# A hybrid DeltaNet and window-attention layer on one core: x transposed before its norm, the first two tiles together, split decays, and the last rows stored one by one

## The chip, the cores and the metric

One core of one Trainium2 chip. The metric is the device time of one execution in microseconds (us); the numbers given for a kernel are medians over several executions. TensorE is the matrix engine (PE in the profile; its weight loads are PEld), VectorE is DVE, ScalarE is ACT, GpSimd is POOL, SyncE is SP. SP issues the weight transfers; ScalarE issues the transfers of x, the constants and the output.

## The reference: what is computed

```python
h = rms_norm(x, norm_w)                       # x: 2048 x 1024, fp32
z = h @ w_in                                  # all branches' inputs
# branch A: gated DeltaNet, 8 heads of 128, chunks of 64
q, k, v = silu(causal_conv(z_qkv)); q, k = l2_normalize(q), l2_normalize(k)
g = -exp(a_log) * softplus(a + dt_bias)
gc = cumsum(g) within a chunk
decay = exp(gc[i] - gc[j]) for i >= j         # per head and chunk
o = chunked delta rule(q, k, v, decay, beta)
ya = (rms_norm(o) * silu(z_a)) @ w_o_a
# branch B: window attention, 16 heads of 64, sinks, relative bias
yb = (attention(q, k, v) * silu(z_b)) @ w_o_b
y = x + (sigmoid(gate_a) * ya + sigmoid(gate_b) * yb) @ w_out
out = rms_norm(y, final_norm_w)
```

## The kernel before, in words

The sequence is done in 4 blocks of 512 tokens (`TB`), each as 4 rows of 128 (`NT`); the model width of 1024 is 8 slices of 128 (`KT`). Every fp32 operand of a large product is held as a high part in fp32r and a low part that is the rest, and a product is three fp32r matmuls (`split_mm`, L1118 to L1122). The weights are 91 tiles of 128 x 1024. In block 0 each tile is read raw by SP (`load_raw`, L344), its high part made by ScalarE (`high_part`, L447), its low part by POOL (`low_part`, L376), and both parts saved to memory; blocks 1 to 3 read the saved parts back. There are three weight slots (`SLOTS`). A 128x512 tile product (`gemm_steps`, L1131) is 8 slices of three matmuls, 24 in all, and takes 24 x 0.227 = 5.45 us; it fills one of two PSUM banks, which must have been read (`z_read`) before it is filled again.

The order of the work is written out by hand, engine by engine; engines meet at semaphores, and an engine that waits holds up all that stands behind it in its own program.

**Front (block 0).** ScalarE issues the load of x (L437) and the constants (L440 to L445), makes the high parts of tiles 0 to 2 (L453), squares x (`square_x`, L475) and makes `nea` (L487). VectorE takes the mean (L776), POOL the power -0.5 (L393), and VectorE scales the four rows of x in place (L779). TensorE then transposes x in 8 slices of four (`transpose_x`, L1158), VectorE evicts each with the norm weight into `h32` (L789), ScalarE makes its high part (`h_high`, L482) and VectorE its low part (`h_low`, L796). TensorE runs the three tiles "pro" one after the other: the first waits slice by slice for h. Between the second and the third it transposes the first one's result for beta and the decays (`beta_decay`).

**Heads.** In `head` (L1196) TensorE's own work for a head is mixed with steps of the next head's six tile products (`fill`). It starts with the sums of the decays: POOL makes `g_up`, the mask UPTO times the head's g (`decays`, L395 to L398), and one fp32 matmul of the mask AFTER by `g_up` gives the exponents (L1207). Its result is waited for by ScalarE (exp, L625) and, as leave to overwrite `g_up`, by POOL. Then come transposes of k and q (L1203), the products k k and k q (L1214), the transposes of v, 8 fill steps, the doubling levels (`square`, `apply`), the logits (L1267) of the attention, whose block-diagonal q (`qbd`) ScalarE wrote in the head before (L566, L567) into one of two buffers, and the four chained steps of the state. The head's output is transposed in L1348, just ahead of the next head's L1207.

**Block ends.** After the heads come 16 gate tiles (6 inside the last head), 8 "ya", 8 "yb", 3 "pro" and 8 "out" tiles. ScalarE issues the load of the next block's x after the last head and squares it after gate tile 8; VectorE scales it; TensorE transposes 6 slices after gate tile 14 and 2 within "ya" (L1380 to L1388).

**Tail.** The last 8 tiles give 4 rows x 2 halves. VectorE adds each half to x (L1101) when the half's last tile is done, ScalarE squares the 4 rows (L754), VectorE takes the mean (L1107), POOL the power, VectorE scales the rows (L1110), and one 2 MB transfer stores them (L760).

## Time and profile before

| | us |
|---|---|
| median of 3 runs | 2855.15 (2854.82 to 2855.34) |
| the profiled execution | 2855.39 |
| its span, first to last instruction | 2853.6 |
| TensorE busy | 2779.8 (97%) |
| VectorE busy | 1408.7 (49%) |
| ScalarE busy | 956.1 (34%) |
| POOL busy | 410.5 (14%) |
| TensorE's mean granted clock | 0.997 |
| transfers | 463.12 MB, 162 GB/s |

The span leaves out 1.8 us of the execution around it. Times in the trace count from the span's start. "Busy" is the union of the recorded instructions; matmuls overlap each other, so their pace is read from the distance of their starts, not from their durations. In a row of the timeline the bracket at the end says how long the engine had sat idle before it and which instruction ended that.

### The profile page before, as it was taken

How to read it: one execution, taken by the hardware profiler on the slowest of the kernel's cores; microseconds unless marked ns; L12 is line 12 of the kernel's file. 1: busy time of each engine (PE TensorE's matmuls, PEld its weight loads, DVE VectorE, ACT ScalarE, POOL GpSimd, SP SyncE). 2: the span in 40 equal slices, each digit the busy share in tenths (PEclk: the TensorE clock that was granted, in tenths of full speed). 3: DMA queues.
4: the chain of work that ended last, by engine and by line, in shares of the span. 5: the costliest groups of instructions: out<-in, count | busy, mean ns of one | idle time of the engine just before them, and what ended most of it. 6: DMA issues, size and time to landing. Idle time of an engine off the chain costs nothing.

```text
span 2853.6 us, 48812 instructions
## 1 busy us (share of the span) xinstructions
PE 2779.8 (97%) x19624; PEld 2279.9 (80%) x19624; DVE 1408.7 (49%) x3173; ACT 956.1 (34%) x2961; POOL 410.5 (14%) x237
## 2 busy tenths in 40 slices
PE   5999999999999999999999999999999999999997
PEld 4877777788888888888888888888888888888885
DVE  4577667523166666622226666652224666664022
ACT  3444444432233434331113434432112344333100
POOL 3333233343201000100001000100000001100000
PEclk9999999999999999999999999999999999999998
DMA  6545444488643333345553323325555233323553
GB/s 218 186 162 185 140 158 159 171 306 317 237 166 123 106 116 113 119 164 216 195 215 122 116 106 121 123 105 192 209 189 210 106 121 121 108 107 118 202 207 137
DMA packets 77552, 463.12 MB, mean 162 GB/s; under 512 B 13072, under 2 KB 17296, under 8 KB 29200
## 3 DMA queue, kind: packets, MB, share of 16 engines
q1 hardware_dynamic: 65520, 429.42, 42.1%
q10 hardware_dynamic: 11808, 30.57, 2.9%
q8 instruction: 157, 2.57, 0.4%
q14 instruction: 67, 0.55, 0.1%
HBM read 356.15 MB, written 103.81 MB: 161 GB/s over the span
## 4 chain that ended last, share of the span: by engine, by line
PE 84%; issue 8%; DVE 5%; POOL 1%; ACT 1%; DMA 1%; DVEq 0%; POOLq 0%; SPq 0%; ACTq 0%
PE bank L1120 21%; PE bank L1122 20%; PE bank L1121 20%; PE bank L1240 5%; PE bank L1229 3%; PE bank L1267 2%; PE bank L1214 2%; PE bank L1282 1%; PE bank L1203 1%; PE bank L1274 1%; PE bank L1330 1%; PE bank L1335 1%; PE bank L1325 1%; PE bank L1320 1%; PE bank L1338 1%
## 5 line engine op out<-in xcount | busy, mean ns | idle before, releaser
L1120 PE MATMUL bank<-hT_hi,w_sl 128*128 128x512 f32 x2144 | 904.7, 422 | 12.2 <-DVE za L854 10.7
L1122 PE MATMUL bank<-hT_hi,w_sl 128*128 128x512 f32 x2144 | 840.3, 392 | 0.0
L1121 PE MATMUL bank<-hT_lo,w_sl 128*128 128x512 f32 x2144 | 837.7, 391 | 0.0
L1120 PEld LDWEIGHTS bank<-hT_hi,w_sl 128*128 128x128 f32 x2144 | 404.0, 188 | 92.0 <-issue 23.2
L1122 PEld LDWEIGHTS bank<-hT_hi,w_sl 128*128 128x128 f32 x2144 | 402.3, 188 | 89.8
L1121 PEld LDWEIGHTS bank<-hT_lo,w_sl 128*128 128x128 f32 x2144 | 405.1, 189 | 58.4
L380 POOL TENSOR_TENSOR w_sl<-w_raw,w_sl 128x1024 fp32r<-128x1024 f32 x91 | 229.0, 2519 | 455.1 <-ACT w_sl L453 455.0
L872 DVE SCALAR_TENSOR_TENSOR area<-zraw,stc,area 128x512 f32<-128x512 f32 x288 | 234.5, 814 | 3.3
L393 POOL TENSOR_TENSOR rqo<-qo,half 128x8 f32<-128x8 f32 x32 | 52.4, 1638 | 1017.0 <-DVE qo L1023 1017.0
L771 DVE TENSOR_SCALAR area<-bank 128x256 f32<-128x256 f32 (+1 forms) x192 | 81.0, 422 | 237.9 <-PE bank L1240 196.8
L1240 PE MATMUL bank<-area 64*64 64x128 f32 (+1 forms) x3072 | 162.4, 245 | 0.0
L1006 DVE SCALAR_TENSOR_TENSOR s_cur<-s_cur,scs,bank 128x128 f32<-128x128 f32 x128 | 44.4, 347 | 230.7 <-PE bank L1335 230.7
L617 ACT ACTIVATE area<-bank 128x256 f32<-128x256 f32 x160 | 61.5, 384 | 253.2 <-PE bank L1229 253.0
L1240 PEld LDWEIGHTS bank<-area 64*64 64x64 f32 x3072 | 134.7, 134 | 11.7 <-issue 11.7
L1229 PEld LDWEIGHTS bank<-area 64*64 64x64 f32 x2560 | 87.1, 134 | 58.0 <-issue 54.8
L453 ACT ACTIVATE w_sl<-w_raw 128x1024 fp32r<-128x1024 f32 x91 | 96.1, 1056 | 77.6 <-PE bank L1122 47.7
L541 ACT ACTIVATE zraw<-bank 128x512 f32<-128x512 f32 x96 | 56.8, 591 | 170.6 <-PE bank L1122 167.7
L1070 DVE SCALAR_TENSOR_TENSOR area<-area,bank 128x512 f32<-128x512 f32 x28 | 19.3, 688 | 185.9 <-PE bank L1122 185.9
L536 ACT ACTIVATE area<-area 128x512 f32<-128x512 f32 x96 | 60.0, 625 | 149.7 <-DVE area L872 149.7
L1229 PE MATMUL bank<-area 64*64 64x64 f32 x2560 | 109.0, 224 | 0.3 <-ACT area L621 0.3
L667 ACT ACTIVATE o_sb<-bank,scs 128x128 f32<-128x128 f32 x128 | 46.7, 365 | 170.1 <-PE bank L1325 170.0
L1120 PE MATMUL bank<-w_sl,oa_hi 128*128 128x512 f32 x256 | 100.6, 393 | 0.0
(192 smaller groups left out, 4565.0 us busy)
## 6 DMA issues: line engine op xcount, KB each, us to landing
w_sl<-saved_w SPq DMA_DIRECT2D x273, 1024.0 KB, 4.8
saved_w<-w_sl SPq DMA_DIRECT2D x91, 1024.0 KB, 4.8
w_raw<-in_w_tiles SPq DMA_DIRECT2D x91, 512.0 KB, 5.9
area<-in_x ACTq DMA_DIRECT2D x8, 2048.0 KB, 10.0
out_y<-area ACTq DMA_DIRECT2D x4, 2048.0 KB, 7.2
bias_sb<-in_bias ACTq DMA_DIRECT2D x33, 128.0 KB, 3.1
fw<-in_final_w ACTq DMA_DIRECT2D x1, 512.0 KB, 10.5
stc<-in_step_const ACTq DMA_DIRECT2D x32, 6.5 KB, 2.4
```

Source lines behind the costliest of these rows:

```text
L380: pool.tensor_tensor(w_sl[:, s, 1, :], w_raw[:, f % 2, :], w_sl[:, s, 0, :].bitcast(F32), ALU.subtract).then_inc(lo_ready, 1)
L453: act.activation(w_sl[:, s, 0, :], w_raw[:, f % 2, :], ACT.Copy).then_inc(hi_ready, 1)
L536: act.activation(ez[i % 2], qkv[:, par, i, :], ACT.Tanh, scale=0.5).then_inc(tanh_z[i], 1)
L617: act.activation(p_sb[l % 2], pv(bank[5]), ACT.Copy).then_inc(p_ready, 1)
L771: return dve.tensor_scalar(dst, src, 1.0, None, ALU.mult)
L872: ins = dve.scalar_tensor_tensor(acc, zraw[:, i, k:k + TB], stc[:, par, CONV * i + k:CONV * i + k + 1], acc, ALU.mult, ALU.add)
L1120: pe.matmul(dst, a_hi, b_hi, start=first, stop=False)
L1121: pe.matmul(dst, a_hi, b_lo, start=False, stop=False)
L1122: return pe.matmul(dst, a_lo, b_hi, start=False, stop=last)
L1214: ins = pe.matmul(dst[:, t, :], k[:, c], src[:, c], start=True, stop=True)
L1229: ins = pe.matmul(pv(bank[5])[lo:hi, t, :], ptt[lo:hi, t, 0:CH], p_sb[(l - 1) % 2][lo:hi, t, :], start=True, stop=True)
L1240: ins = pe.matmul(bch(6)[lo:hi, t, c0:c1], p_sb[(l - 1) % 2][lo:hi, t, :], ptt[lo:hi, t, c0:c1], start=True, stop=True)
```

## The change

x comes in four loads of one row each, for block 0 two from SP (ahead of the weights) and two from ScalarE. TensorE transposes the raw x. The reciprocal root is put on a diagonal (`diag_x`, VectorE), multiplied by the mask of ones (`rstd_broadcast`, one fp32 128x512 matmul into bank 7), copied to SBUF by ScalarE (`rstd_rows`) and multiplied in when `h32` is evicted. The transposes use five banks instead of six. In the front the squares come first, the first two tiles are computed together, slice by slice, and the constants' loads shrink to four. g is split into `g_hi` and `g_lo`; POOL makes two masked products, and two fp32r matmuls take the place of the fp32 one. `qbd` has one buffer instead of two. In the last block, rows are added, squared, scaled and stored one by one.

```diff
-        qbd = sb("qbd", [P, 2, NC, P])
+        qbd = sb("qbd", [P, NC, P])
+        after_r = sb("after_r", [P, P], F32R)
+        g_hi = sb("g_hi", [P, NT, H], F32R)
+        g_lo = sb("g_lo", [P, NT, H])
+        gu = sb("gu", [P, 2, NT, P], F32R)
...
-        g_up = chunks(scratch(0))
+        g_up = [gu[:, 0, :, :], gu[:, 1, :, :]]
-        junk_q, junk_k = chunks(scratch(7)), chunks(scratch(9))
+        junk_q, junk_k = chunks(scratch(4)), chunks(scratch(9))
+        zflat = zraw[:, :, :].rearrange("p i t -> p (i t)")
+        diag_x = chunks(zflat[:, 0:TB])
+        rstd_x = zflat[:, D:D + TB]
...
SP:
+            for t in (2, 3):
+                sp.dma_start(x_sb[:, t, :], x[0][:, t, :]).then_inc(x_landed[t], 16)
             load_raw(0)
             load_raw(1)
POOL:
-            def decays(par, n1):
+            def decays(h, n1):
                 pool.wait_ge(sc_ready, n1)
-                pool.tensor_tensor(g_up, mk[:, UPTO:UPTO + 1, :].to_broadcast([P, NT, P]),
-                                   scs[:, par, G, :, None].to_broadcast([P, NT, P]), ALU.mult).then_inc(gup_ready, 1)
+                pool.wait_ge(g_split, (n1 - 1) // H + 1)
+                for up, g in zip(g_up, (g_hi[:, :, :].bitcast(F32), g_lo[:, :, :])):
+                    ins = pool.tensor_tensor(up, mk[:, UPTO:UPTO + 1, :].to_broadcast([P, NT, P]),
+                                             g[:, :, h, None].to_broadcast([P, NT, P]), ALU.mult)
+                ins.then_inc(gup_ready, 1)
...
+            power(st4[:, 4:8], st4[:, 8:12], NT, x_mean, 1, x_rstd)
             low(SLOTS)
-            power(st4[:, 4:8], st4[:, 8:12], NT, x_mean, 1, x_rstd)
...
+                    for t in range(NT):
+                        power(sty[:, 4 + t:5 + t], sty[:, 8 + t:9 + t], 1, row_mean, t + 1, row_rstd)
ScalarE:
+            def load_x(j, ts=range(NT)):
+                for t in ts:
+                    act.dma_start(x_sb[:, t, :], x[j][:, t, :]).then_inc(x_landed[t], 16)
+            load_x(0, (0, 1))
             act.dma_start(mk[:, :, :], masks).then_inc(const_in, 16)
...
-            act.dma_start(bias_sb[:, 0, :, :], bias[0]).then_inc(const_in, 16)
-            act.dma_start(fw[:, :], final_w).then_inc(const_in, 16)
-            for n in range(SLOTS):
-                high_part(n)
...
+            def rstd_rows(j):
+                act.wait_ge(bc_done, j + 1)
+                act.activation(rstd_x, bank[7][:, :], ACT.Copy).then_inc(bc_ready, 1)
             square_x(0)
+            high_part(0)
+            high_part(1)
+            rstd_rows(0)
+            for k in range(KT):
+                h_high(0, k)
+            high_part(2)
...
             act.activation(nea[:, :], db[:, 0, :], ACT.Exp).then_inc(const_ready, 1)
+            act.dma_start(fw[:, :], final_w).then_inc(fw_in, 16)
...
+                after(act, lg_done[1], n1 - 1)
+                act.activation(qbd[0:DH, :, 0:CH], zq[0:DH], ACT.Copy, scale=DH ** -0.5)
+                act.activation(qbd[DH:P, :, CH:P], zq[DH:P], ACT.Copy, scale=DH ** -0.5).then_inc(z_read[bk], 1)
...
+                act.wait_ge(ssq_ready[0], n1)
                 p_copy(0)
                 act.wait_ge(ksc_ready, n1)
                 scaled(kd, bch(3), ksc, kd_ready)
-                act.wait_ge(ssq_ready[0], n1)
...
                     if more and j == FILL_GATES + 2:
                         square_x(b1)
+                if more:
+                    rstd_rows(b1)
...
+                if not more:
+                    for t in range(NT):
+                        act.wait_ge(half_added, t + 1)
+                        act.activation(junk_y[:, 0:TB], y_out[:, t, 0:TB], ACT.Square, accum_out=sty[:, 12 + t:13 + t]).then_inc(row_ssq, 1)
+                        act.wait_ge(row_ssq, t + 1)
+                    for t in range(NT):
+                        act.wait_ge(row_added, t + 1)
+                        act.activation(junk_y[:, TB:D], y_out[:, t, TB:D], ACT.Square, accum_out=sty[:, t:t + 1]).then_inc(row_ssq, 1)
+                        act.wait_ge(row_ssq, NT + t + 1)
+                    for t in range(NT):
+                        act.wait_ge(row_final, t + 1)
+                        act.dma_start(out[b][:, t, :], y_out[:, t, :]).then_inc(y_stored, 16)
+                    break
VectorE:
                 dve.wait_ge(x_rstd, j + 1)
-                for t in range(NT):
-                    ins = dve.tensor_scalar(x_sb[:, t, :], x_sb[:, t, :], st4[:, 4 + t:5 + t], None, ALU.mult)
-                ins.then_inc(x_normed, 1)
+                dve.tensor_tensor(diag_x, mk[:, IDENT:IDENT + 1, :].to_broadcast([P, NT, P]),
+                                  st4[:, 4:8, None].to_broadcast([P, NT, P]), ALU.mult).then_inc(x_diag, 1)
...
+                dve.wait_ge(bc_ready, j + 1)
-                dve.tensor_scalar(h32[k % 2], bank[2 + k % 6][:, :], nw[:, k:k + 1], None, ALU.mult).then_inc(h32_ready, 1)
+                dve.scalar_tensor_tensor(h32[k % 2], bank[2 + k % 5][:, :], nw[:, k:k + 1], rstd_x, ALU.mult, ALU.mult).then_inc(h32_ready, 1)
...
+            dve.tensor_scalar(after_r[:, :], mk[:, AFTER, :], 1.0, None, ALU.mult).then_inc(dve_init, 1)
...
+                ch.link(dve.tensor_scalar(g_hi[:, :, :], sc_all[:, G, :, :], 1.0, None, ALU.mult))
+                dve.tensor_tensor(g_lo[:, :, :], sc_all[:, G, :, :], g_hi[:, :, :].bitcast(F32), ALU.subtract).then_inc(g_split, 1)
...
+                    for t in range(NT):
+                        add(t, 0, half_added)
+                        if t == 1:
+                            dve.wait_ge(half_added, 2)
+                    for t in range(NT):
+                        if t < NT - 1:
+                            dve.wait_ge(out_part, t + 1)
+                        else:
+                            dve.wait_ge(tile_done, USE["out", b, 2 * NT - 1] + 1)
+                        add(t, 1, row_added)
+                        if t:
+                            mean(t - 1)
+                        if t > 1:
+                            final(t - 2)
+                    mean(NT - 1)
+                    final(NT - 2)
+                    final(NT - 1)
+                    break
TensorE:
+            def rstd_broadcast(j):
+                pe.wait_ge(x_diag, j + 1)
+                pe.matmul(bank[7][:, :], mk[:, ONES, :], diag_x.rearrange("p t c -> p (t c)"), start=True, stop=True
+                          ).then_inc(bc_done, 1)
...
-                pe.matmul(bank[5][:, :], mk[:, AFTER, :], g_up.rearrange("p t c -> p (t c)"), start=True, stop=True
+                pe.matmul(bank[5][:, :], after_r[:, :], g_up[0].rearrange("p t c -> p (t c)"), start=True, stop=False)
+                pe.matmul(bank[5][:, :], after_r[:, :], g_up[1].rearrange("p t c -> p (t c)"), start=False, stop=True
                           ).then_inc(dec_done, 1)
...
-            pe.wait_ge(x_normed, 1)
+            for k in range(5):
+                transpose_x(0, k)
+            rstd_broadcast(0)
+            n = USE["pro", 0, 0]
+            pair = (gemm_steps(n, hT_hi, hT_lo), gemm_steps(n + 1, hT_hi, hT_lo))
             for k in range(KT):
-                transpose_x(0, k)
-            n = USE["pro", 0, 0]
-            gemm(n, hT_hi, hT_lo, True)
-            gemm(n + 1, hT_hi, hT_lo)
+                if k < KT - 5:
+                    transpose_x(0, k + 5)
+                pe.wait_ge(h_hi, k + 1)
+                pe.wait_ge(h_lo, k + 1)
+                for steps in pair:
+                    next(steps)
+            for steps in pair:
+                next(steps, None)
...
                     if more and j == GATE_TILES - 2:
-                        pe.wait_ge(x_normed, b + 2)
-                        for k in range(6):
+                        pe.wait_ge(ot_read, (b + 1) * H)
+                        for k in range(5):
                             transpose_x(b + 1, k)
+                        rstd_broadcast(b + 1)
...
-                    if more and c in (1, 2):
+                    if more and c < KT - 5:
                         transpose_x(b + 1, c + 5)
```

## Rows read from the trace of the kernel before

**Rows 1.** Page, part 4: the chain that ended last, by engine.

```profile
PE 84%; issue 8%; DVE 5%; POOL 1%; ACT 1%; DMA 1%; DVEq 0%; POOLq 0%; SPq 0%; ACTq 0%
```

**Rows 2.** Windows: heads of block 0 and of block 1 (stretch: length, busy of each).

```profile
88.00:565.00 477.00, 456.40 (x3818) 369.18 (x3817) 322.95 (x689) 223.00 (x700) 164.37 (x79) 1.00 0.47 161
807.00:1260.00 453.00, 452.52 (x3821) 370.19 (x3820) 272.40 (x690) 179.69 (x652) 41.18 (x31) 1.00 0.32 115
```

**Rows 3.** Waits of PE: two of block 0's heads, the only one of block 1's.

```profile
PE bank L1120 <- DVE za L854: 10.7, 7, 1.5
PE bank L1330 <- DVE r_sb L1000: 5.1, 8, 1.7
...
PE bank L1335 <- ACT y_sb L670: 0.5, 1, 0.5
```

**Rows 4.** Timeline of the front (start us, us, what, idle before).

```profile
19.38 1.06 ACT L453 ACTIVATE w_sl<-w_raw 128x1024 fp32r<-128x1024 f32 x1 [6.21 <-DMA w_raw<-in_w_tiles]
20.34 1.04 ACT L475 ACTIVATE zraw<-area 128x1024 f32<-128x1024 f32 x1
20.51 2.35 POOL L380 TENSOR_TENSOR w_sl<-w_raw,w_sl 128x1024 fp32r<-128x1024 f32 x1 [4.93 <-ACT w_sl L453]
25.12 0.17 DVE L776 TENSOR_SCALAR st<-st 128x4 f32<-128x4 f32 x1 [25.12 <-ACT zraw L475]
29.31 5.89 PE L1158 MATMUL bank<-mk,area 128*128 128x128 f32 x32 [29.31 <-DVE area L779]
30.51 0.75 DVE L789 TENSOR_SCALAR za<-bank,nw 128x512 f32<-128x512 f32 x1 [1.27 <-PE bank L1158]
...
40.20 0.63 ACT L482 ACTIVATE hT_hi<-zb 128x512 fp32r<-128x512 f32 x1
40.87 0.69 DVE L796 TENSOR_TENSOR hT_lo<-zb,hT_hi 128x512 fp32r<-128x512 f32 x1
...
48.33 0.48 PE L1120 MATMUL bank<-hT_hi,w_sl 128*128 128x512 f32 x1
```

**Rows 5.** DMA view of the first 60 us: rate in 40 slices, issues to landing.

```profile
GB/s 0 248 377 385 404 395 406 240 295 360 279 254 429 426 355 93 437 188 336 0 0 0 0 0 0 0 0 0 0 0 11 126 399 197 328 262 339 205 334 1
...
w_raw<-in_w_tiles SPq DMA_DIRECT2D x7, 512.0 KB, 6.0
area<-in_x ACTq DMA_DIRECT2D x1, 2048.0 KB, 9.5
```

**Rows 6.** Timelines of DVE and ScalarE's queue in the tail.

```profile
2833.31 2.48 DVE L1101 TENSOR_TENSOR area<-bank,area 128x512 f32<-128x512 f32 x4 [19.42 <-PE bank L1122]
...
2841.84 4.87 DVE L1110 SCALAR_TENSOR_TENSOR area<-area,sty,fw 128x1024 f32<-128x1024 f32 x4 [1.12 <-POOL sty L393]
...
2846.80 0.35 ACTq L760 DMA_DIRECT2D out_y<-area  x1
```

**Rows 7.** Timeline of PE at the start of a head of block 1.

```profile
1146.46 0.60 PE L1348 MATMUL bank<-mk,area 128*128 128x128 f32 x4
1146.90 1.02 PE L1207 MATMUL bank<-area,mk 128*128 128x512 f32 x2
1147.76 1.04 PE L1203 MATMUL bank<-mk,area 128*128 128x128 f32 x8
...
1153.16 0.39 PE L1121 MATMUL bank<-hT_lo,w_sl 128*128 128x512 f32 x1
1153.39 0.39 PE L1122 MATMUL bank<-hT_hi,w_sl 128*128 128x512 f32 x1
```

**Rows 8.** Timeline of POOL and DVE in the same head.

```profile
1157.37 1.04 POOL L397 TENSOR_TENSOR area<-mk,scs 128x512 f32<-128x512 f32 x1 [4.13 <-DVE scs L771]
1157.44 1.26 DVE L868 TENSOR_SCALAR area<-zraw,stc 128x512 f32<-128x512 f32 x1
...
1160.81 0.42 DVE L771 TENSOR_SCALAR area<-bank 128x256 f32<-128x256 f32 x1 [2.12 <-PE bank L1240]
```

**Rows 9.** Timeline of DVE at the start of a head of block 0.

```profile
147.98 2.73 DVE L1042 TENSOR_TENSOR oa_lo<-za,oa_hi 128x512 fp32r<-128x512 f32 x1
```

107 lines of the change are left out of this document (68 added, 39 removed).

## The prediction, made blind

> **What bounds the kernel now.** I read the page first: in the chain that ended last TensorE holds 84% [rows 1]. A share like that hides which stages have slack, so next comes the table by stage [rows 2]. In block 1's heads (807 to 1260 us) TensorE works 452.52 of 453 us; in block 0's heads (88 to 565) only 456.40 of 477. So there are three kinds of time: the front before the first product and the tail after the last, where TensorE idles; block 0, where it waits for others; and the rest, where only TensorE's own work counts. The waits say for whom block 0 waits: VectorE's SiLU of za 10.7 us in 7 waits, r_sb 5.1 us in 8; block 1 has 0.5 us in all [rows 3].
>
> A change of less than 0.2% (5.7 us) is no change for a measurement of this kernel.
>
> **Front.** Today ScalarE converts weight tile 2 (19.38) before it squares x, because its program has the conversions first; x has long landed: its load takes 9.5 us from its issue at 0.74 [rows 4, 5]. Then four squares from 20.34, the mean at 25.12, power, the four scalings of x, transposes from 29.31, the first h32 at 30.51, the last low part of h ends at 41.56, both first tiles are done at about 48, and tile 2 starts at 48.33 [rows 4].
>
> After the change the step is built up as follows.
> - x: the same 2 MB, now ahead of the weights on both queues. The DMA slices run at some 380 to 400 GB/s [rows 5], so 2 MB take about 5.3 us of transfer. I estimate the first quarter at 6.8 and the last at 9.3 us; the bounds are 5 and 10.3 (today's landing of the whole).
> - Four squares take 25.12-20.34 = 4.8: from 6.8 to 11.6; I take 12.
> - Mean 0.2, power 1.0, one 128x512 product on VectorE 0.7, one fp32 128x512 matmul 0.9 (priced below), one ScalarE copy 0.6, and 0.1 for each of five hand-overs: 3.9, so the first h32 comes at 16. ScalarE's two weight conversions (2 x 1.06) fit into the time in which it waits for that matmul. The raw transposes of slices 0 to 4 are done by then. POOL now does the power ahead of all low parts, so low part 1 ends near 18.2.
> - Eight slices take 41.56-30.51 = 11.05 us [rows 4]: VectorE sets the pace at 1.38 us a slice. The eviction becomes a scalar_tensor_tensor with one PSUM and one SBUF input; its nearest row is 0.69 against 0.75 now (the residual add, 2.48 for four, a pitch of 0.6 [rows 6]), so I count no change. I add 1 us, since low part 1 on POOL now overlaps the chain and VectorE can be stretched by POOL (below). End: 28.
> - The pair of tiles eats six matmuls a slice, 6 x 0.227 = 1.36 us, just VectorE's pace, so both tiles end 1.4 us later, 29.5. Today the second tile needs 5.45 us more, after the first.
> - What is late next: tile 2's weights. Its conversion stands behind the last h_high on ScalarE, so 27.3+1.06 = 28.4, and its low part takes 2.4 (L380) after a short hand-over: 30.9. Tile 2 starts at 31.0, and I allow 0.5 us for TensorE's start: **31.5 instead of 48.33, a gain of 16.8 us.**
>
> That allowance is the soft spot. TensorE's granted clock is 1.00 throughout the front, yet its 32 first transposes take 5.9 us, 0.18 us each, where four later ones take 0.44, 0.11 each [rows 4, 7]: 2 us are lost after the idle 29 us. If it starts at half pace once more between the transposes and the gemm, the pair lags up to 2.5 us, since six matmuls a slice at half pace cost 2.7 us against VectorE's 1.38; the lower bound takes that in. The Trainium skill ("TensorE: Matmul & The Clock Gate", What's actually happening) says that an idle array falls back to 1.2 GHz and needs sustained work to rise again. By that rule the pair would start at 1.2 GHz and tile 2 at about 33. The first transposes agree with it; no row shows a short gap.
>
> The front's gain holds only if the following weights keep up: raw tile 4 is issued after low part 2 (31.3), lands 6.0 later [rows 5], is converted and split by 40.8, and is wanted at 31.5+2 x 5.45 = 42.4. It fits by 1.6 us. After that TensorE is bound as before to its 88.15. Bounds of the whole: 13 and 20 us.
>
> **Decays.** One fp32 matmul 128x512 (two records) holds TensorE from L1207 at 1146.90 to L1203 at 1147.76: 0.86 us. An fp32r matmul of the same shape starts every 0.227 us (1153.16, 1153.39) [rows 7]. Two of those are 0.455, saving **0.40 us a head.** I cost the change of type before and after at nothing, since the gemm's matmuls stand between fp32 ones at every turn already. In blocks 1 to 3 TensorE has no slack, so 24 heads give 9.7.
>
> POOL pays: two 1.04 products a head instead of one. VectorE feels it: an L868 that begins beside POOL's L397 takes 1.26 us and ends 0.3 us after it; a second product holds it 1.04 us longer. But VectorE then sits idle for 2.12 us before its next step [rows 8], which covers it. At a block's start nobody waits for the product today: block 1's list has no such wait [rows 3]. The Trainium skill ("GPSIMD Engine Reference", Specifications) has the two engines share their SBUF interfaces, in contention when VectorE's instruction has two SBUF inputs or a 2-port mode. By that rule L868 loses 1.04 us in all 24 heads; the sum stays the same while the idle 2.12 us cover it.
>
> In block 0 seven heads wait at the first fill matmul for VectorE (1.5 us each) [rows 3]. VectorE's delay starts at the output transposes, ahead of the decay matmul, so those heads gain nothing; head 0 gains 0.4. There the second product falls where VectorE reads PSUM, so I cost it at zero. Sum for decays: **10.0 us**, bounds 6 (each block 0 head loses half of a product) and 13 (all 32 gain).
>
> **Block boundaries.** VectorE's four scalings go, one product, one ScalarE copy, three more DMA issues come; all hidden, since TensorE does nine gate tiles of 5.45 us between the load's issue and its first transposes and never waits there. The new wait for the broadcast row stands ahead of h32, which is wanted only by the next "pro" tiles, dozens of microseconds later. TensorE has one more fp32 128x512 matmul: 3 x 0.86 = **2.6 us lost.** Transposes stay 32, five slices ahead and three later. The single qbd buffer adds a wait on ScalarE for the second logits of the head before; in its program order it already waited for later work (probs of the second half), so zero. The ssq_ready wait ahead of p_copy is for ScalarE's own older work: zero.
>
> **Tail.** TensorE ends at T = 2833.3, where VectorE's wait ends; today four adds (2.48), four squares, mean and power (to 2841.84), four finals (4.87), then a 2 MB store issued at 2846.80 and ended with the span at 2853.6: 20.3 us [rows 6]. Afterwards only row 3 is left at T: add 0.7, then VectorE's mean of row 2 and final of row 1 to T+2.3, mean of row 3 to 2.75, final of row 2 to 3.95 (its power is ready at 2.4), final of row 3 (power ready at 3.9) to 5.2. The 512 KB store: 2 MB take 6.8 us, less 1.5 MB at 400 GB/s that is 2.9; a raw tile of 512 KB behind another transfer takes 6.0 [rows 5]. I take 3.7, nearer the first, since only row 2 is ahead of it. Started at 5.3 it lands at T+9.0. **Gain 11.3 us**, bounds 9 and 12.1. TensorE's own halt for the first half's adds shrinks by 0.1.
>
> **Sum.** 16.8 + 10.0 - 2.6 + 11.3 = 35.5 us off the profiled execution's 2855.39, which stands 0.24 over the median of the runs: 2819.9, so **2820 us**.
>
> **Rivals.**
> - The front is held by DMA and a slow TensorE: x lands late, weights arrive late, gain 10 instead of 16.8: 2827. For it: the landing is 9.5 us at nearly full DMA shares. 15%.
> - Block 0 gains too: less waiting on VectorE's chain because everything there shifts; 7 x 0.4 more, and the front at 18: 2816. 12%.
> - fp32r is no cheaper here (0.43 each, as the fp32 records): the change doesn't do what it says, and 10 us are missing: 2830. Against it the 0.227 of all other fp32r matmuls. 2%.
> - POOL's second product is not covered: each head loses a full 1.04 us, 32 x 1.04 = 33: 2853, no change. Against it the 2.12 us. 4%.
> - Slower: the same place, but POOL and VectorE stretch each other. It decides at a delay of 2.12+35.5/32 = 3.2 us a head; at 3.7 a head loses 1.6, 51 us in all: 2871. For it: in block 0 a VectorE subtraction takes 2.73 instead of 0.69 (the front's h low part has it) while POOL's low parts run [rows 9]. Against it: L397 is a third as long as two low parts. 2%.
>
> My forecast has the remaining 65%. The range holds it and the first three rivals, as well as the bounds summed, 13+6-2.6+9 = 25.4 to 20+13-2.6+12.1 = 42.5 us of gain: 2812 to 2830. Faster: 65+15+12+2 = 94%; within 0.2%: 4%; slower: 2%.
>
> **What would show it.** Tile 2's start near 31.5; L1207's records half as wide, the next transposes 0.46 us after them, and a head's period in blocks 1 to 3 shorter by 0.4; block 0's wait for za longer by 0.4; L868 at 2.3 us without a new wait of TensorE; store of row 3 at T+5.3. I am wrong if TensorE shows new waits in blocks 1 to 3, or if weights stop it between 31 and 88 us.

## The result: 2833.5 us instead of 2855.2, and where the forecast's other 13.5 us went

| | before | after |
|---|---|---|
| median | 2855.24 (2854.82 to 2855.52, 4 runs) | 2833.51 (2827.68 to 2836.23, 4 runs) |
| ratio | | 0.9921, 95% interval 0.9909 to 0.9933 |
| the profiled execution, its span | 2855.39, 2853.6 | 2835.45, 2833.6 |

The change makes the kernel faster by 21.7 us. The forecast was 2820 with a range of 2812 to 2830: the sign was right, the size was not. The four runs of the changed kernel also lie 8.5 us apart, those of the kernel before 0.7. That spread is the first clue: something in the new kernel comes out now one way and now the other. TensorE's mean granted clock goes with it: 0.998 in the run of 2827.68, 0.997 in that of 2831.58, 0.996 in the other two, 2835.45 and 2836.23. The profiled execution is thus one of the slower ones.

The page of the changed kernel, parts 1 and 4:

```profile
PE 2783.0 (98%) x19632; PEld 2288.2 (81%) x19632; DVE 1406.3 (50%) x3177; ACT 958.6 (34%) x2973; POOL 450.7 (16%) x272
...
PE 92%; DVE 4%; ACT 1%; issue 1%; DMA 1%; POOL 1%; ACTq 0%; DVEq 0%; SPq 0%
```

TensorE holds 92% of the chain instead of 84% [rows 1], as it should where front and tail shrink. But its busy time rose from 2779.8 to 2783.0, although the decay matmuls became cheaper. Busy time of an engine that does less can only rise if some of its work ran slower.

**Where the 20.0 us of the span came from.** I compared the start of the decay matmul of each head (L1207 before, L1303 after). It is earlier by 10.9 us in head 0, 11.35 in head 1 and 11.37 in head 2, and then the lead melts: 9.98, 8.60, 8.65, 7.27 and 5.61 in heads 3 to 7 of block 0, and 2.81 at the first head of block 1 (804.39 against 807.20). From there it grows by 0.38 in most heads, loses 0.6 at each of the two block boundaries, and is 8.9 at TensorE's last matmul; the tail adds 11.1.

| | forecast | measured in the profiled executions |
|---|---|---|
| front, to the third tile | 16.8 | 10.9 |
| block 0, from its first decay matmul to block 1's (with the first boundary) | 0.4 - 0.9 | -8.1 |
| blocks 1 to 3, with two boundaries | 9.7 - 1.7 | 6.1 |
| tail | 11.3 | 11.1 |
| sum | 35.5 | 20.0 |

**Block 0.** The view of PE's waits between 77 and 555 us of the changed kernel:

```profile
PE bank L1211 <- DVE za L908: 13.8, 7, 2.2
PE bank L1427 <- DVE r_sb L1054: 5.0, 8, 1.7
```

The wait for za is 13.8 us in 7 instead of 10.7 [rows 3], 0.44 a head longer. That is the forecast's own term: the cheaper decay matmul of these heads is waited away. But 7 x 0.4 only explains that nothing is gained. The rest is in the windows by stage (length, busy of PE, PEld, DVE, ACT, POOL, granted clock, DMA share, GB/s):

```profile
77.20:550.00 472.80, 451.48 (x3757) 367.49 (x3756) 315.17 (x677) 219.03 (x690) 168.27 (x84) 0.98 0.46 159
...
198.00:200.50 2.50, 0.64 (x3) 0.58 (x4) 2.50 (x4) 1.84 (x12) 2.50 (x2) 1.00 0.50 206
200.70:203.00 2.30, 2.30 (x8) 1.79 (x7) 1.48 (x4) 0.00 (x0) 1.99 (x2) 0.56 1.08 235
```

Block 0's mean granted clock (the number ahead of the DMA share, which stands second from the end) is 0.98, where it was 1.00 [rows 2]; in block 1 it is 1.00. In the head that starts at 194 us it reads 1.00 while TensorE idles, then 0.56. In matmuls, from PE's timeline of the same head:

```profile
199.86 0.47 PE L1211 MATMUL bank<-hT_hi,w_sl 128*128 128x512 f32 x1 [1.94 <-DVE za L908]
...
202.05 0.63 PE L1212 MATMUL bank<-hT_lo,w_sl 128*128 128x512 f32 x1
202.48 0.63 PE L1213 MATMUL bank<-hT_hi,w_sl 128*128 128x512 f32 x1
```

From 201.2 to 204.2 the matmuls start 0.43 us apart, and from 204.5 on 0.23 again: TensorE runs at 1.2 GHz for 3 us, 1.3 us after an idle of 1.94 us has ended. The head is then 61.08 us long instead of 59.66; three others are as long (61.06 to 61.35), and the last one loses as much. The kernel before idled 1.53 us at the same place and its clock read 1.00 there. So the saving of 0.4 us did not merely come to nothing; it made the idle longer (1.91 to 2.21 us), and in five of seven heads the longer idle was followed by some 3 us at half pace; in the two others, after idles of 1.92 and 1.91, it was not. At this point that is a reading of one trace, and it is what the first experiment tests.

The idle itself is VectorE's and POOL's. Their timelines in that head:

```profile
195.94 5.42 POOL L401 TENSOR_TENSOR w_sl<-w_raw,w_sl 128x1024 fp32r<-128x1024 f32 x2 [3.82 <-ACT w_sl L480]
201.67 1.38 POOL L414 TENSOR_TENSOR rk<-ssk,half 128x4 f32<-128x4 f32 x1 [0.31 <-DVE ssk L955]
```

```profile
196.38 2.73 DVE L1096 TENSOR_TENSOR oa_lo<-za,oa_hi 128x512 fp32r<-128x512 f32 x1
199.04 0.68 DVE L908 SCALAR_TENSOR_TENSOR za<-area,bank 128x512 f32<-128x512 f32 x1
```

VectorE's oa_lo is 2.73 as before [rows 9], and za, for which TensorE waits, stands right behind it. The arithmetic is telling: the first of POOL's two low parts ends near 195.94 + 2.4 = 198.3, and oa_lo, which takes 0.69 undisturbed, ends 0.7 after that. It did not run slower, it stood until POOL's instruction was over. The SiLU of za, which has one input in PSUM, takes 0.68 beside the second low part. The Trainium skill ("SBUF — State Buffer", SBUF: two separate sides) says just that: whichever of the two engines starts first holds the shared ports for its whole instruction, and the other blocks. The trace agrees, 2.73 against 0.69.

**Front.** The timelines of ScalarE, POOL, VectorE and PE, in order of time:

```profile
10.21 1.06 ACT L499 ACTIVATE zraw<-area 128x1024 f32<-128x1024 f32 x1 [2.17 <-DMA area<-in_x]
13.97 4.53 PE L1254 MATMUL bank<-mk,area 128*128 128x128 f32 x20 [13.97 <-DMA db<-in_decay_bias]
14.48 1.02 POOL L414 TENSOR_TENSOR st<-st,half 128x4 f32<-128x4 f32 x1 [10.75 <-DVE st L826]
15.47 5.10 POOL L401 TENSOR_TENSOR w_sl<-w_raw,w_sl 128x1024 fp32r<-128x1024 f32 x2
15.54 2.83 DVE L828 TENSOR_TENSOR zraw<-mk,st 128x512 f32<-128x512 f32 x1 [1.21 <-POOL st L414]
18.43 1.92 PE L1243 MATMUL bank<-zraw,mk 128*128 128x512 f32 x2
21.08 0.75 DVE L839 SCALAR_TENSOR_TENSOR za<-bank,nw,zraw 128x512 f32<-128x512 f32 x1 [2.71 <-ACT zraw L505]
...
31.32 0.69 DVE L846 TENSOR_TENSOR hT_lo<-zb,hT_hi 128x512 fp32r<-128x512 f32 x1
...
37.43 0.48 PE L1211 MATMUL bank<-hT_hi,w_sl 128*128 128x512 f32 x1
```

The first h32 comes at 21.08, forecast 16. Row 1 of x landed only at 10.2, so the squares end 2 us late; the diagonal is 2.83 instead of 0.7, since POOL's low part began 0.07 us ahead of it; the broadcast is 1.92 instead of 0.9, at half pace. From the first h32 to the last low part it takes 10.9, as forecast (11.05, and 1 allowed). But then the pair of tiles is not done: it began at 23.3, ran at half pace to about 26.4 and ended at 36.9, so the third tile starts at 37.43, forecast 31.5.

**Blocks 1 to 3** behave mostly as forecast (6.1 instead of 8.0). PE at the start of the head at 1141 us:

```profile
1141.42 0.60 PE L1445 MATMUL bank<-mk,area 128*128 128x128 f32 x4
1141.78 0.48 PE L1303 MATMUL bank<-gu,after_r 128*128 128x512 f32 x1
1142.10 0.39 PE L1304 MATMUL bank<-gu,after_r 128*128 128x512 f32 x1
1142.33 1.04 PE L1299 MATMUL bank<-mk,area 128*128 128x128 f32 x8
```

From L1303 to the next transposes it is 0.55, where it was 0.86 [rows 7], and 0.36 instead of 0.44 from L1445 to L1303: 0.39 a head together. POOL's second product and VectorE beside it:

```profile
1152.33 1.05 POOL L420 TENSOR_TENSOR gu<-mk,g_hi 128x512 fp32r<-128x512 f32 x1 [4.12 <-issue]
1153.34 1.23 POOL L420 TENSOR_TENSOR gu<-mk,g_lo 128x512 fp32r<-128x512 f32 x1
```

```profile
1152.40 1.25 DVE L922 TENSOR_SCALAR area<-zraw,stc 128x512 f32<-128x512 f32 x1
1155.40 0.42 DVE L821 TENSOR_SCALAR area<-bank 128x256 f32<-128x256 f32 x1 [1.74 <-PE bank L1337]
```

VectorE's product is stretched by the first of POOL's two and by no more than before [rows 8]: 1.25, not the 2.3 that were forecast, and 1.26 at most in all heads of blocks 1 to 3. It idles 1.74 us afterwards, and TensorE has no new wait. What is missing there is the seventh head of each of these blocks, 0.35 us longer in its state steps for a reason that I did not find, and 0.34 us of a late weight load in block 3.

**Tail.** The timelines of VectorE and of ScalarE's queue around TensorE's last matmul, which ends at 2824.4:

```profile
2823.94 1.28 DVE L1164 SCALAR_TENSOR_TENSOR area<-area,sty,fw 128x1024 f32<-128x1024 f32 x1
2825.13 0.69 DVE L1154 TENSOR_TENSOR area<-bank,area 128x512 f32<-128x512 f32 x1
```

```profile
2826.66 3.89 ACTq L800 DMA_DIRECT2D out_y<-area  x4
```

The final of row 0 begins just before TensorE ends and holds the last add back by 0.7 us; still the span ends 9.2 us after TensorE, instead of 20.3 [rows 6].

### The profile page after: what moved, and what is told of

Same layout as the page of the kernel before. It is cut to its first block, busy times and chain, and to the rows that moved or that the text cites. A ratio compares the mean times of both kernels' runs of the same rounds, so it can differ in the third digit from the quotient of the medians.

```text
span 2833.6 us, 48983 instructions
## 1 busy us (share of the span) xinstructions
PE 2783.0 (98%) x19632; PEld 2288.2 (81%) x19632; DVE 1406.3 (50%) x3177; ACT 958.6 (34%) x2973; POOL 450.7 (16%) x272
## 4 chain that ended last, share of the span: by engine, by line
PE 92%; DVE 4%; ACT 1%; issue 1%; DMA 1%; POOL 1%; ACTq 0%; DVEq 0%; SPq 0%
PE bank L1211 24%; PE bank L1213 22%; PE bank L1212 22%; PE bank L1337 5%; PE bank L1326 3%; PE bank L1364 2%; PE bank L1311 2%; PE bank L1379 1%; PE bank L1371 1%; PE bank L1299 1%; PE bank L1427 1%; PE bank L1432 1%; PE bank L1417 1%; PE bank L1422 1%; PE bank L1435 1%
## 5 line engine op out<-in xcount | busy, mean ns | idle before, releaser
L1211 PE MATMUL bank<-hT_hi,w_sl 128*128 128x512 f32 x2144 | 909.2, 424 | 14.7 <-DVE za L908 13.8
L414 POOL TENSOR_TENSOR sty<-sty,half 128x1 f32<-128x1 f32 (+1 forms) x7 | 7.1, 1020 | 612.9 <-DVE sty L1198 424.8
L1211 PE MATMUL bank<-oa_hi,w_sl 128*128 128x512 f32 x256 | 100.6, 393 | 0.0
```

The lines of the kernel that those rows point to most:

```text
L414: pool.tensor_tensor(dst, src, half[:, 0:n], ALU.pow).then_inc(ready, 1)
L1211: pe.matmul(dst, a_hi, b_hi, start=first, stop=False)
```

## The experiments

The question was what holds block 0 and the front back. Theory C: the longer idle of TensorE lets the granted clock fall. Its rivals: the cost of the decays' own parts, POOL's queue, or VectorE's order of work. All ran beside the kernel before, whose median was 2855.5 to 2855.7 each time; ratios are to it, of four executions unless it is said otherwise. A median alone says little here where the clock varies: the changed kernel's own runs reach from 2827.7 to 2836.2. So the traces decide.

### 1. Two spare matmuls in block 0's heads

```diff
                 pe.wait_ge(gup_ready, n1)
+                if 1 < n1 <= H:
+                    for _ in range(2):
+                        pe.matmul(bank[5][:, :], after_r[:, :], g_up[0]..., start=True, stop=True)
```

> The changed kernel with two extra fp32r matmuls ahead of the decay matmuls in heads 1 to 7 of block 0, whose result is overwritten. Theory C (TensorE's clock): in block 0 the 0.40 us saved by the decay matmuls only lengthens TensorE's idle time ahead of the first fill matmul (1.53 to 1.94 us), and after the longer idle its granted clock falls to half in most of these heads, at 1.4 us each. The pads give the 0.45 us back to work that was idle anyway: wait back to 1.5 us, no half-pace matmuls, heads of block 0 59.7 us apart, time some 6.5 us below the changed kernel (about 2827), spread of the runs below 2 us. Rival P (POOL): the second masked product on POOL delays block 0 and the pads change nothing or add 7 x 0.45 = 3 us: 2833 to 2837, spread as before.

Measured: **2828.7** (2827.3 to 2831.6), ratio 0.9909 (0.9893 to 0.9926). TensorE does more work, and the median is 4.8 us lower. The runs of the two kernels overlap, and the spread of 4.3 us is more than the 2 that I expected, so the comparison has to be made head by head. PE's waits between 88 and 550 us, and the window behind the idle of the same head:

```profile
PE bank L1211 <- DVE za L908: 10.5, 7, 1.7
```

```profile
200.50:203.00 2.50, 2.50 (x13) 2.07 (x12) 1.56 (x4) 0.00 (x0) 2.26 (x2) 1.00 0.93 254
```

In this head the idle is 1.46 us, the clock stays at 1.00, and the heads are 59.7 us apart. From block 0's first head to block 1's it is 721.1 us, with the change as it is 727.2, and in run 1 no clock falls there: some 6 us were the clock's in that execution. (The profiled execution of run 1 is its fastest, that of the change one of its slower ones.) The later traces bear theory C out: over all kept traces whose idle for za is 1.90 us or more (the change, runs 2, 5, 6, 7 and 8) the clock fell in 23 of 42 such heads; where it is 1.43 to 1.81 (before, runs 1, 3 and 9), in none of 28. What decides among the longer ones, no run shows.

This trace shows a second thing. Its front is the same code as the changed kernel's, yet its third tile starts at 34.85 instead of 37.43. The window of the pair's first matmuls in the changed kernel:

```profile
24.00:26.00 2.00, 2.00 (x6) 1.41 (x6) 1.96 (x4) 1.26 (x2) 0.00 (x0) 0.50 0.96 406
```

and in run 1:

```profile
24.00:26.00 2.00, 2.00 (x14) 1.69 (x13) 1.96 (x4) 0.87 (x2) 0.00 (x0) 1.00 0.96 406
```

In one execution the pair runs its first 3 us at 1.2 GHz, in the other at 2.4. Of the 2.6 us, 0.2 are the constants' landing (13.77 instead of 13.97), 0.8 the broadcast (1.15 instead of 1.92) and 1.6 the pair: all but the first are chance of the clock. Head 0 gives 1.0 of them back: there TensorE waits 1.22 us for another product of VectorE's, and the head is 58.23 us long instead of 57.23. The Trainium skill ("TensorE: Matmul & The Clock Gate", What's actually happening) says that the length of the cold stretch differs between runs of one kernel; the two traces agree. This, and the heads of block 0 whose clock falls or doesn't, is where the changed kernel's spread comes from as far as the granted clocks of the runs tell.

### 2 and 3. The decays alone, and everything but the decays

Run 2 is the kernel before with g split, two products of POOL, two fp32r matmuls and one qbd buffer; run 3 the changed kernel with the decays as before:

```diff
-                pe.matmul(bank[5][:, :], after_r[:, :], g_up[0]..., start=True, stop=False)
-                pe.matmul(bank[5][:, :], after_r[:, :], g_up[1]..., start=False, stop=True
+                pe.matmul(bank[5][:, :], mk[:, AFTER, :], g_up..., start=True, stop=True
```

> The kernel before with the split decays and the single q buffer alone. Theory C: blocks 1 to 3 gain 0.39 us a head (24 heads, 9.3 us, less about 1 in the seventh heads), block 0 gains 0.4 in head 0 and then loses 1.4 us in each head where the clock falls, in about 5 of 7: 2855.2 - 0.4 - 8.3 + 7 = 2853.5, runs several us apart. Rival P: POOL's second product costs the same in every head of all blocks, so no head of blocks 1 to 3 would be shorter than 56.6 us: 2855 or more. If the clock does not fall here: 2846.5.

> The changed kernel with the fp32 decay matmul and one POOL product. Theory C: the wait ahead of the fill is 1.53 us again and the clock stays up in the heads of block 0 (59.68 us apart); front gains 10.9, tail 11.1, the boundaries cost 3 x 0.89, late weights 0.8: 2855.2 - 22.0 + 3.5 = 2836.7, spread under 1 us. If the front's shift alone made the clock fall in block 0, heads there would be 61 us apart and the time 2843.

Measured: decays alone **2852.98** (2849.28 to 2854.04, 10 runs), ratio 0.9990 (0.9981 to 0.9999); all but the decays **2837.09** (2836.5 to 2837.34), ratio 0.9935 (0.9920 to 0.9950). Both lie within 0.6 us of what was expected. The decays, forecast at 10.0, bring 2.6 alone and 3.6 on top of the rest; and wherever they are, the runs scatter (4.8 us in run 2), and where they are not, they don't (0.8). The ten runs of run 2 go by their granted clock: 2849.28 at 0.996, 2851.2 to 2853.1 at 0.995, 2853.7 to 2854.0 at 0.994. In run 2 four heads of block 0 are 61.0 us long, in run 3 none is, its wait for za being 11.0 us in 7, nearly as before the change (10.7).

### 4. VectorE does za and zb before oa

```diff
-                fill(2)
+                fill(3)
                 dve.wait_ge(ot_done, n1)
```

> The changed kernel with VectorE's SiLU of za moved ahead of its evictions of the head's output (oa high and low part), where POOL's low parts stretch it. Theory C: TensorE's wait for za in heads 1 to 7 of block 0 disappears (7 x 1.94 us) and with it the half-pace stretches (about 6.5 us): 2833.5 - 20 = 2813.5, unless another wait takes its place; spread below 2 us; blocks 1 to 3 unchanged. Rival P: the wait remains or moves by POOL's load, 2830 or more.

Measured: **2842.06** (2841.97 to 2844.52), ratio 0.9955 (0.9940 to 0.9970): a miss by 28 us, and 8.5 slower than the change. PE's waits between 88 and 550 us, and the window behind one of them:

```profile
PE bank L1386 <- DVE area L968: 23.0, 7, 3.5
```

```profile
209.00:212.00 3.00, 3.00 (x10) 2.33 (x9) 2.92 (x9) 2.27 (x8) 0.90 (x1) 0.55 0.75 293
```

The wait for za is gone as expected, and the next one, for f (VectorE's products at L968, behind the squares of k and POOL's power rk), has taken its place and is longer (3.3 us a head), since f comes at the end of the same chain and nothing in that chain got shorter. TensorE rests in one piece, the clock fell in this idle or just behind it in all seven heads (0.55 in the window shown), and the heads are 61.9 us apart. What I had missed is that the wait for za and the wait for f are one debt of VectorE's, paid at whichever door comes first.

### 5 and 6. The front: TensorE kept busy; POOL behind the diagonal

`keep_busy(n)` is n fp32 128x512 matmuls of zeros into a bank that is overwritten later.

```diff
             pe.wait_ge(zeroed, 6)
+            keep_busy(9)
+            pe.wait_ge(const_in, 16 * 4)
             for k in range(5):
                 transpose_x(0, k)
+            keep_busy(2)
             rstd_broadcast(0)
+            keep_busy(2)
```

```diff
+            pool.wait_ge(x_diag, 1)
             low(SLOTS)
```

> The changed kernel with 13 extra fp32 matmuls of zeros in the front: 9 before the constants land, 2 behind the transposes and 2 behind the broadcast row, to keep TensorE busy. If TensorE's half pace cost the front 1 us in the broadcast row (1.92 instead of 0.86) and 3.4 us in the first slices of the pair: the transposes take 2.2 instead of 4.5 us, the first h32 comes at 20.0 instead of 21.1, and the third tile starts at 33.8 instead of 37.4, where its low part (33.7) is next. If DMA or VectorE alone set the front, it stays at 37 or comes later by the extra work. The time itself varies by several us with the clock in block 0, so the trace decides; near 2830.

> The changed kernel with POOL's first low parts held back until VectorE has the diagonal. If POOL's two low parts stretched the diagonal from 0.7 to 2.83 us: it takes 0.7, the first h32 comes at 19.0 instead of 21.1; low part 1 ends at 21.4 instead of 20.6 and delays nobody; TensorE still runs at half pace first, third tile at 35.3 to 37.4. If the stretch is VectorE's own: 2.8 us again.

Measured: 5 gives **2829.6** (2828.7 to 2830.5, 2 runs), ratio 0.9909 (0.9889 to 0.9929); 6 gives **2833.7** (2833.3 to 2834.1, 2 runs), ratio 0.9924 (0.9904 to 0.9943). PE in run 5:

```profile
14.00 2.40 PE L1254 MATMUL bank<-mk,area 128*128 128x128 f32 x20 [0.46 <-DMA db<-in_decay_bias]
...
18.45 1.13 PE L1243 MATMUL bank<-zraw,mk 128*128 128x512 f32 x2 [0.33 <-DVE zraw L828]
...
34.67 0.66 PE L1272 MATMUL bank<-mk,zraw 128*128 128x128 f32 x4
```

Kept busy, TensorE does the 20 transposes in 2.40 instead of 4.53 and the broadcast in 1.13 instead of 1.92, and the transposes for beta, just ahead of the third tile, start at 34.67 instead of 37.02. Expected was 33.8 for the tile; it is 35.08. That is no better than the 34.85 which run 1 had by chance, without the added matmuls. VectorE and PE in run 6:

```profile
15.73 0.69 DVE L829 TENSOR_TENSOR zraw<-mk,st 128x512 f32<-128x512 f32 x1 [1.21 <-POOL st L414]
20.30 0.75 DVE L840 SCALAR_TENSOR_TENSOR za<-bank,nw,zraw 128x512 f32<-128x512 f32 x1 [3.87 <-ACT zraw L506]
```

```profile
14.17 4.53 PE L1255 MATMUL bank<-mk,area 128*128 128x128 f32 x20 [14.17 <-DMA db<-in_decay_bias]
18.49 1.07 PE L1244 MATMUL bank<-zraw,mk 128*128 128x512 f32 x2
```

The diagonal is 0.69 again, as expected, but the broadcast starts no earlier (18.49): in TensorE's program the cold transposes stand ahead of it and take until then. In run 5 the transposes are done at 16.4, and there the broadcast waits for the stretched diagonal (18.45). In the change the one ends at 18.4 and the other at 18.5, so taking away either of them alone gains nothing at this place. Run 8 takes away both, and the broadcast still starts at 18.35 and the first h32 comes at 20.11: now the spare matmuls stand ahead of it (the first nine end at 14.6, and two more begin at 16.63). So no run shows how early the broadcast could start. What the spare matmuls change is the chance: in the eight traces with the front as it was or with POOL's part alone moved, the third tile starts between 34.85 and 37.43 (36.39 in run 6), in the three with spare matmuls (5, 8 and 12) between 34.71 and 35.08. The medians of 5 and 6 both lie within the changed kernel's own runs and decide nothing.

### 7 and 8. One of block 0's low parts moved behind dec_n; and all three together

`dec_n` is POOL's product of the decays with a mask, which stands between the power rk and the next low part. Run 8 is runs 5, 6 and 7 in one.

```diff
                                    ALU.mult).then_inc(decn_ready, 1)
-                low(2)
+                low(3 if n1 > 1 else 2)
...
                       qo_ready, n1, rqo_ready)
-                low(2)
+                low(2 if last else 1)
```

> The changed kernel with POOL's power rk put between the two low parts at a head's start in block 0 instead of behind both. The moved SiLU showed that behind the wait for za a second one (output f, 3.5 us) comes due, whose chain goes through rk on POOL. Theory D (POOL's queue bounds block 0's heads): low part 2 and its 2.7 us leave the chain, oa_lo is stretched by one low part at most as before, but f comes 2 us earlier; the wait for za stays at 1.5 to 1.9, the one for f stays at 0. Then nothing more is gained than by the pads: 2828 to 2833. If VectorE is freed earlier as well (its first op behind a low part no longer waits), heads fall to 58 to 59 us and the clock stays up: 2818 to 2824.

> The changed kernel with all three: TensorE kept busy in the front, low parts behind the diagonal, rk between the low parts. Front: h32 at 18.0, pair bound by VectorE, third tile at 31.5 to 33.5 (4 to 6 us gained); block 0 as in the run with rk between the low parts. Sum: 4 to 6 us below that run.

Measured: 7 gives **2837.65** (2837.09 to 2838.43), ratio 0.9937 (0.9920 to 0.9953), and 8 gives **2837.54** (2837.0 to 2837.94), ratio 0.9937 (0.9922 to 0.9952). Both missed. In run 7 VectorE's timeline, PE's waits in block 0 (70 to 560 us) and the window of the first heads show why:

```profile
197.43 2.73 DVE L1096 TENSOR_TENSOR oa_lo<-za,oa_hi 128x512 fp32r<-128x512 f32 x1
...
204.49 2.24 DVE L962 TENSOR_TENSOR bj<-rk,scs 128x4 f32<-128x4 f32 x1
```

```profile
PE bank L1386 <- DVE area L968: 6.1, 4, 1.5
```

```profile
88.00:380.00 292.00, 274.20 (x2335) 222.98 (x2334) 208.10 (x419) 134.73 (x418) 99.74 (x51) 1.00 0.45 154
```

The low part that stayed still blocks oa_lo, and the one that moved blocks bj, a product of 4 columns: 2.24 us instead of 0.16, right ahead of f. All heads from the second on are some 61.1 us apart, but not for the clock alone: in the four heads from 134 to 379 us it stays at 1.00, and TensorE waits 1.5 us for f in each; in the last three the clock falls (at 385, 446 and 508 us), and there is no such wait. The length is the same either way, so here VectorE's chain sets it and half pace costs nothing. Run 8 has the same picture, with five waits for f (7.6 us) and two falls of the clock. In its trace the third tile starts 2.2 us before run 7's and block 1's first head 1.8 before; yet the medians are alike, and run 7's profiled execution was its slowest. What the other executions of run 8 lost, no trace shows.

### 9. The tail alone

The kernel before with the rows added, squared, scaled and stored one by one.

> The kernel before with the tail of the changed kernel alone: rows added, squared, scaled and stored one by one. If the tail's parts are worth what the trace of the changed kernel shows (20.3 us from TensorE's last result to the end became some 9.2), this gives 2855.4 - 11.1 = 2844.3, within 0.5, and a spread as small as that of the kernel before, since block 0 is untouched. If some of the tail's gain came from other parts of the change, it is above 2845.5.

Measured: **2844.24** (2844.13 to 2844.45), ratio 0.9961 (0.9946 to 0.9976). The tail is worth 11.2 us by itself, and the runs lie 0.3 us apart.

### 10. POOL's low parts held until VectorE can't be blocked

```diff
                                    ALU.mult).then_inc(decn_ready, 1)
-                low(2)
+                if n1 <= H:
+                    pool.wait_ge(f_ready, n1)
+                low(3 if n1 > 1 else 2)
...
                       qo_ready, n1, rqo_ready)
-                low(2)
+                if n1 < H:
+                    pool.wait_ge(head_dve_done, n1)
+                low(2 if last else 1)
```

> The changed kernel with POOL's low parts of block 0 held: at the end of a head one low part, and only once VectorE's oa_lo is done; the other two only once the head's f is done. Theory A (block 0 is bound by VectorE's chain, stretched by POOL's low parts at the head's start: oa_lo 2.73 instead of 0.69, and then by rk standing behind them): oa_lo takes 0.7, the wait for za all but goes (13.8 us before), the wait for f stays under 1 us a head, no granted clock falls, the pitch of block 0's heads is 58 us or less instead of 59.7 to 61.1: 2833.5 - 7 x 2 = 2819, within 3. Theory B (the time is only moved: the low parts stretch whatever VectorE does next, as when they were moved behind the mask's product): pitch 61, 2837 as there.

Measured: **2825.63** (2824.71 to 2826.07), ratio 0.9894 (0.9878 to 0.9911). The fastest version of this study, 7.9 us under the change and with a spread of 1.4; its slowest run is below the change's fastest. Against the 2819 of theory A it is a miss of 6.6 us. VectorE's timeline and PE's waits between 88 and 550 us:

```profile
194.96 0.69 DVE L1100 TENSOR_TENSOR oa_lo<-za,oa_hi 128x512 fp32r<-128x512 f32 x1
...
202.66 2.95 DVE L977 TENSOR_TENSOR area<-area,mk 64x256 f32<-64x256 f32 x2
```

```profile
PE bank L1330 <- ACT area L660: 8.8, 7, 1.8
```

oa_lo takes 0.69, and the wait for za has all but gone, as theory A has it. But the pitch was expected at 58 us or less, and the heads are 59.2 to 59.5 apart (one 61.3): a new wait of 8.8 us stands at the first squaring of P, and behind it the clock fell once (the head of 61.3). VectorE's product for ptt (L977, two instructions), blocked to 2.95 by the held low part, looks like the cause of the wait.

### 11 and 12. The same, held longer; and with the warm front

```diff
-                    pool.wait_ge(f_ready, n1)
+                    pool.wait_ge(attn_ready, n1)
```

> As the run before this one, but POOL's two held low parts wait for VectorE's attn instead of f, which is 2 to 3 us later. There the first of them stretched VectorE's product for ptt (0.85) to 2.95, and TensorE waited 8.8 us in 7 waits at its first squaring of P. If block 0 is bound by VectorE's chain wherever a low part lies on it, that wait goes too and each of seven heads is 1.0 to 1.5 us shorter: 2825.6 - 7 x 1.3 = 2816.5, within 3. If the time only moves, a new wait (the low part of the second next tile comes late, or r_sb grows) takes its place: 2825 or more.

> The same with the front's two additions: matmuls of zeros that keep TensorE busy while it waits for x (their results are overwritten), and POOL's low parts behind the diagonal. The third tile began 2.3 us earlier with these. If block 0 no longer gives that back through its granted clock, this is 2 us below the run beside it: 2814.5. If it does give it back, the two are within 0.7.

Measured: 11 gives **2829.51** (2828.95 to 2830.99), ratio 0.9909 (0.9893 to 0.9926); 12 gives **2828.55** (2828.28 to 2828.97), ratio 0.9905 (0.9891 to 0.9920). The first is a miss: 13 us above the 2816.5 hoped for and 4 slower than run 10, which was the other case written down. PE's waits, ScalarE, VectorE and a window in run 11:

```profile
PE bank L1330 <- ACT area L660: 8.9, 8, 1.9
...
PE bank L1330 <- DVE area L825: 4.3, 5, 1.0
```

```profile
205.87 1.06 ACT L484 ACTIVATE w_sl<-w_raw 128x1024 fp32r<-128x1024 f32 x1 [2.29 <-DMA w_raw<-in_w_tiles]
```

```profile
203.44 0.85 DVE L977 TENSOR_TENSOR area<-area,mk 64x256 f32<-64x256 f32 x2
```

```profile
210.00:212.00 2.00, 2.00 (x13) 1.13 (x11) 1.50 (x3) 1.20 (x5) 0.22 (x1) 0.50 1.10 276
```

ptt takes 0.85 again and is ready at 204.3, and the wait of 8.9 us is still there, so ptt was not what held it. ScalarE stands at 205.87 in front of a raw weight tile that has not landed, and the copies that TensorE waits for are behind it in ScalarE's program. SP issued that tile's load at 199.31, as soon as POOL's held low part had freed its raw buffer (there are two), and it took 6.5 us. In the change as it was the same load was issued at 198.97 and nobody wanted it before 207; now VectorE's chain is faster than the weights. Run 10 has the same wait of ScalarE for the raw tile (2.24 us, conversion at 205.05). Held longer, the other two low parts also block two instructions of VectorE's that stand ahead of its copies of P (2.27 us for a copy of 20 columns, 2.35 for one product), which is the second wait shown (4.3 us); run 10 had 0.4 of it. So the next bound of block 0 is the supply of raw tiles. That is read from the trace; a third raw buffer was not tried. Behind the 1.86 us idle of this head the clock is 0.50 once more. Run 12 starts its third tile 1.7 us before run 11 and ends 1.0 before it, between the two cases that were written down: head 0 gives 1.5 us back (58.66 instead of 57.20), and no clock falls in block 0, where run 11 has one fall.

## Why the prediction was wrong, step by step

- **The front** (forecast 16.8, measured 10.9, outside the bounds of 13 and 20). The step that failed first is the landing of x: the rows came in pairs, 0 and 2 at 6.7 to 6.9, 1 and 3 at 9.8 to 10.1. The whole of x landed no earlier than before, and since ScalarE squares the rows in order, three squares stood behind row 1 and ended at 13.7 instead of 12; the sum had let them run without a break. It also left the constants out, which come in the same stretch of time and without which neither the transposes nor VectorE start (13.97). Next came the chain at 3.9 us: measured 14.17 to 21.08, 6.9, with 2.1 in the diagonal and 1.0 in the broadcast. I had the rule for the first in hand (a VectorE subtraction takes 2.73 beside a low part [rows 9]) and applied it to L868 but not to this product. Runs 5 and 6 then show that diagonal and cold transposes held the broadcast equally: each alone keeps it at 18.45 or 18.49. Last, "the pair lags up to 2.5 us": it did, and since the pair began at 23.3 and needs 10.9 us at full pace, it and not the weights set the third tile's start. Run 1's trace has 13.5 for the same front with the pair at full pace, just inside the bounds: 3.3 us were missing from the chain itself and 2.6 came and went with the clock and the constants' landing. The first rival (gain 10) was right about the size and about two of its reasons, the late x and the slow TensorE; the weights were not late (their last low part ended at 34.7), and the diagonal was not in it; 15% was too little for what the text itself called the soft spot.
- **Block 0** (forecast 0.4, measured -7.2 without the boundary). "Those heads gain nothing" was right as a sum of instructions: the saved 0.4 us is found again in the wait for za. The step that failed is the silent one behind it, that a longer idle costs nothing. Run 1 shows that it costs: with work added, block 0 is 6.1 us shorter between the two profiled executions. No rival had this; all of them let time move between engines, and none let TensorE's own pace depend on where its idle lies, although the front's first transposes had shown it and the text had priced it there.
- **Blocks 1 to 3** (forecast 9.7 and -2.6). 0.39 a head against 0.40, boundaries -0.89 each against -0.86. Right in the sum. But the second product's 1.04 us on VectorE, which the forecast counted and found covered, did not come at all (1.25 instead of 2.3), so that the cover was not put to the test; 1.4 us are missing in three heads and one weight load. (By their own terms the decays are 10.1, not 10.0.)
- **Tail** (forecast 11.3). 11.1 in the trace, 11.2 by itself in run 9. Right, though row 0's final delays the last add, which the working did not have.
- **The range** ended at 2830 because the bounds were added only where I had seen a doubt. In the profiled executions the front is 5.9 us short of its forecast, block 0 with its boundary 7.6, blocks 1 to 3 with theirs 1.9 and the tail 0.2; that is 15.5 to rounding, and the profiled execution of the change lies 1.9 above its median. How often the clock falls decides a good part of it: one of the four executions took 2827.68, inside the range, so that both the miss and its size are partly chance.

## What to carry to other kernels

Before a saving is counted at zero because another engine is waited for, look at what it does to the idle time: a shorter instruction ahead of a wait lengthens the idle, and TensorE may come back at half pace. Then look at who sets the length of that stretch: in run 7 half pace cost nothing, since VectorE's chain was as long. Where a kernel's own runs lie 8.5 us apart, compare traces stage by stage and each run's granted clock, not two medians. Where one engine's wait goes, ask which other wait is fed by the same chain (za and f here), and shorten the chain rather than reorder its ends. Bulk work on POOL belongs where VectorE has nothing to do in SBUF, and even then only as long as it doesn't starve the buffers that it frees.

## What was not expected of the hardware

- An idle of 1.94 us in a stream of matmuls was followed, about 1 us after it ended, by some 3 us at 1.2 GHz; 1.53 us (before) and 1.46 us (run 1) at the same place were not. Nor was every longer one: after idles of 1.90 us or more for za the clock fell in 23 of 42 heads, and in run 4, whose idles are 3.2 us and more, in seven of seven. The same in run 10, at another place of the head: behind an idle of 1.82 us the clock fell to 0.50 (head of 61.3 us), behind one of 1.19 it did not (59.5), nor in run 12 behind one of 1.88.
- The same front ran its pair of tiles at either level in different executions; with the broadcast before it the third tile was 2.6 us apart (34.85 and 37.43).
- A VectorE product of 4 columns took 2.24 us instead of 0.16 when a low part of POOL began just ahead of it. The product ended at 206.73, the low part at 204.33 + 2.38 = 206.71: what was lost here was not set by the size of VectorE's instruction but by what was left of POOL's.
